# A fourth K pair by seven products in the first iteration of both down stages

## The chip, the cores and the metric

The kernel runs on one core of a Trainium2 chip. The metric is the device time of one execution in microseconds (us). Engines are named as the profile names them: PE is TensorE (PEld its weight loads), DVE is VectorE, ACT is ScalarE, POOL is GpSimd, and SP issues the weight DMAs.

## What is computed

One layer of a macaron decoder block on 256 tokens of width 2048, all in float32. The part that the change touches is the second half of each SwiGLU, the product with `w_down` (5632 x 2048), which occurs twice, in `ffn1` and `ffn2`:

```python
def swiglu(x, w_up, w_down):
    g, u = jnp.split(x @ w_up, 2, axis=-1)
    return (jax.nn.silu(g) * u) @ w_down

h = h + 0.5 * rms_norm(swiglu(rms_norm(h, ffn1_pre[l]), ffn1_up[l], ffn1_down[l]), ffn1_post[l])
...
h = h + 0.5 * rms_norm(swiglu(rms_norm(h, ffn2_pre[l]), ffn2_up[l], ffn2_down[l]), ffn2_post[l])
```

## The kernel before

**Three products for one.** PE works on rounded operands (`fp32r`). Each float32 operand is split into a rounded part (`_hi`, written by ACT) and the rest (`_lo`, written by DVE as raw minus hi), and a product is three matmuls: hi x hi, hi x lo, lo x hi (lines 779 to 781, or `three`, lines 870 to 872).

**Groups.** Weights arrive in groups of 256 rows (two K tiles of 128) by 512 columns, 512 KB each, into four slots of `w_raw`; group n uses slot n % 4. For each group SP issues the load (line 572) once DVE has split the group four earlier; ACT rounds it (`w_hi`, line 1260) once PE is through with the group four earlier; DVE takes the rest (`w_lo`, line 1641); PE multiplies it with both token tiles (2 K tiles x 2 token tiles x 3 = 12 matmuls of 128x128 by 128x512). ACT, DVE and SP each work through their own program in order. In the loops of ACT and DVE, step n splits group n+4.

**The down stage.** `down0` and `down1` have two iterations (i = 0, 1). One iteration computes two strips of 512 output columns, A and B, over all 22 pairs k of K tiles, in 44 groups; a tuple per iteration, `DOWN_A` and `DOWN_B`, says at which group number which pair is taken for strip A or B. Steps 40 to 43 of an iteration go tile by tile.

**Quads.** For the pairs named in `DOWN_QUADS`, as (group of A, group of B, k), the four 2x2 block products of strips A and B are done by seven block products in place of eight (`down_products`, lines 927 to 975): 7 x 3 = 21 matmuls where two plain groups take 24. The price is on DVE and ACT. At DVE step ng-4, `down_sum13` (line 1850, 128x1024) waits for `t_used`, that is for PE's last product of the quad before, since there is a single `dt_raw`, `dt_hi`, `dt_lo`; then come the weight split of group ng and `down_sum24` (lines 1858 and 1860, 128x512 each). The split of group nu is only 512 wide. Steps ng-3 and ng-2 each have a `dt_lo` of 128x1024 (line 1906), behind ACT's `dt_hi` (line 1399). PE waits for the first `dt_lo` before its product into bank3, for the second before that into bank2:

```python
pe.wait_ge(t_split, 2 * down_quad(f, i, j) + 1)
p7 = three(bank[3][:, :], *s(2), *tt(1), first, last)
p5 = three(bank[1][:, :], *s(0), *tt(0), first, last)
pe.wait_ge(t_split, 2 * down_quad(f, i, j) + 2)
p6 = three(bank[2][:, :], *s(1), *tt(2), first, last)
```

**The activations' splits.** The hidden activations (`act_raw`) come in 11 strips p of 512, strip p serving pairs k = 2p and 2p+1. `HIDDEN[0]` says at which step of the first iteration a strip is split: ACT writes `act_hi` (line 1341, two instructions), DVE `act_lo` (line 1680, two instructions). For strips 8, 9 and 10 (`D_STRIPS`, the strips of the quads) DVE first forms four sums (`hidden_sums`, lines 1873 to 1876), and a step later ACT and DVE split those (`ds_hi` line 1382, `ds_lo` line 1882). A product of pair k waits on `hid_split` for strip k//2. DVE's order within a step (lines 1896 to 1913):

```python
if n + SLOTS in DQ_A[i]: down_sum13(f, i, DQ_A[i][n + SLOTS])
rest_group(sec, i, n)
if n + SLOTS in DQ_A[i]: down_sum24(f, i, DQ_A[i][n + SLOTS])
if n in DT_AT[i]: ...            # dt_lo
if n in HIDDEN[i]: ...           # hidden_sums for strips 8, 9, 10, then hidden_lo
if n - 1 in HIDDEN[i] and HIDDEN[i][n - 1] in D_STRIPS: hidden_sums_lo(f, HIDDEN[i][n - 1])
```

After the last quad DVE combines the banks (`d_u`, lines 1917 to 1925), and at step `A_LAST` it reads strip A's accumulators (lines 1928 and 1929).

Of the kernel before, what the change touches and what calls it, by code (L numbers as in the profile page):

```python
# [62 lines left out]
def numbered(first, ks):  # L63

    return {first + j: k for j, k in enumerate(ks)}


DOWN_QUADS = (((24, 25, 16), (29, 30, 17), (33, 34, 18)),
              ((4, 5, 16), (9, 10, 17), (14, 15, 18), (18, 19, 19), (22, 23, 20), (26, 27, 21)))
DOWN_A = ({**numbered(0, range(4)), **numbered(8, (4, 5)), **numbered(12, (6, 7)), **numbered(16, (8, 9)),  # L70
           **numbered(20, (10, 11)), **numbered(26, (12, 13)), **numbered(31, (14, 15)), **numbered(35, (19, 20, 21))},
          {**numbered(0, (8, 9, 10)), **numbered(6, (12, 13, 14)), 11: 15, 12: 11, **numbered(28, range(8))})
DOWN_B = ({**numbered(4, range(4)), **numbered(10, (4, 5)), **numbered(14, (6, 7)), **numbered(18, (8, 9)),
           **numbered(22, (10, 11)), 28: 12, **numbered(38, (13, 14, 15, 19, 20, 21))},
          {3: 8, 13: 9, **numbered(16, (10, 11)), **numbered(20, (12, 13)), **numbered(24, (14, 15)), **numbered(36, range(8))})
A_LAST = tuple(max(a) for a in DOWN_A)
HIDDEN = ({2: 2, 5: 3, 8: 4, 11: 5, 13: 6, 15: 7, 18: 8, 24: 9, 32: 10}, {})
D_STRIPS = (8, 9, 10)
D_K0 = 2 * D_STRIPS[0]
NDK = 2 * len(D_STRIPS)  # L80
NDQ = sum(map(len, DOWN_QUADS))

# [69 lines left out]
def hybrid_trunk(nc, t, out):  # L152
# [17 lines left out]
    with ctx:  # L170
# [313 lines left out]
        def down_quad(f, i, j):  # L484

            return NQUAD * NST * (f + 1) + NDQ * f + sum(map(len, DOWN_QUADS[:i])) + j

# [5 lines left out]
        QUAD_UP = {nu: j for j, (ng, nu, k) in enumerate(QUADS)}  # L493
        DQ_A = [{ng: j for j, (ng, nu, k) in enumerate(quads)} for quads in DOWN_QUADS]
        DQ_B = [{nu: j for j, (ng, nu, k) in enumerate(quads)} for quads in DOWN_QUADS]
        T_SLOT = (1, 0, 1)
# [17 lines left out]

        DT_AT = [{ng - 3 + pair: (j, pair) for j, (ng, nu, k) in enumerate(quads) for pair in range(2)} for quads in DOWN_QUADS]

# [51 lines left out]
        def _(sp):  # L568
# [40 lines left out]
            def down_loads(f):  # L609
                for i in range(CH // 2):  # L610
                    source = {n: (k, 0) for n, k in DOWN_A[i].items()}
                    source.update({n: (k, 1) for n, k in DOWN_B[i].items()})
                    for ng, nu, k in DOWN_QUADS[i]:
                        source[ng], source[nu] = (k, 0), (k, 1)
# [633 lines left out]
        def _(act):  # L1248
# [89 lines left out]
            def hidden_hi(f, p):  # L1338
                wait_turned_in(act, f, p)
                for m in range(MT):  # L1340
                    last = act.activation(act_tile(act_hi, p, m), raw_tile(p, m), ACT.Copy)
                last.then_inc(hid_rounded, 1)
# [35 lines left out]
            def sums_hi(f, p):  # L1378

                j = 2 * D_STRIPS.index(p)  # L1380
                act.wait_ge(ds_summed, len(D_STRIPS) * f + D_STRIPS.index(p) + 1)
                act.activation(ds_hi[:, :, j:j + 2, :], ds_raw[:, :, j:j + 2, :], ACT.Copy).then_inc(ds_rounded, 1)
# [7 lines left out]
            def down_strips(f, i):  # L1390

                sec, final = f"down{f}", i == CH // 2 - 1
                for n in range(2 * GF - SLOTS):
                    round_group(sec, i, n)
                    if n in DT_AT[i]:
# [3 lines left out]
                        act.activation(dt_hi[:, both, :], dt_raw[:, both, :], ACT.Copy).then_inc(t_rounded, 1)  # L1399
                    if n in HIDDEN[i]:  # L1400
                        hidden_hi(f, HIDDEN[i][n])
                    if n - 1 in HIDDEN[i] and HIDDEN[i][n - 1] in D_STRIPS:
                        sums_hi(f, HIDDEN[i][n - 1])
                    if n == DOWN_QUADS[i][-1][0]:
# [223 lines left out]
        def _(dve):  # L1628
# [233 lines left out]
            def hidden_sums(f, p):  # L1862

                j, pairs = 2 * D_STRIPS.index(p), 2
                wait_turned_in(dve, f, p)

                def s(y):
                    return ds_raw[:, y, j:j + pairs, :].rearrange("p j (q i) -> p j q i", i=SQ)

                def a(m, kk):  # L1870
                    return raw_tile(p, m)[:, kk:2 * pairs:2]

                link(dve.tensor_tensor(s(0), a(1, 0), a(1, 1), ALU.subtract))
                link(dve.tensor_tensor(s(1), s(0), a(0, 0), ALU.subtract))
                dve.tensor_tensor(s(2), a(0, 0), a(1, 0), ALU.subtract)
                dve.tensor_tensor(s(3), a(0, 1), s(1), ALU.add).then_inc(ds_summed, 1)
# [13 lines left out]
            def down_strips(f, i):  # L1890
# [4 lines left out]
                for n in range(2 * GF - SLOTS):  # L1895
# [5 lines left out]
                    if n in DT_AT[i]:  # L1901
# [5 lines left out]
                                          ALU.subtract).then_inc(t_split, 1)  # L1907
                    if n in HIDDEN[i]:
                        if HIDDEN[i][n] in D_STRIPS:
                            hidden_sums(f, HIDDEN[i][n])  # L1910
# [410 lines left out]
```

## Time and profile before

| what | us |
|---|---|
| three runs, median (lowest to highest) | 2372.98 (2372.71 to 2373.5) |
| the profiled execution | 2372.41 |
| its span, first to last instruction | 2370.6 |
| PE busy in the span | 2356.8 (99%) |
| DVE busy | 1750.5 (74%) |
| ACT busy | 1243.2 (52%) |

The profile is of one execution; its span leaves out 1.8 us around the instructions. The first iteration of `down0` runs from 472.5 to about 591 us of the span, that of `down1` from 2128.7 to about 2247. In the timelines a matmul's row lasts 0.39 us from its start to its modelled end, but the next one starts 0.23 us after it. A DVE row's duration likewise reaches over the start of the next.

### The profile page before, as it was taken

Reading aid. Unit: us, or ns where it says so; the run is one execution under the profiler, and the core shown is the slowest. Engines: PE = TensorE matmul, PEld = TensorE weight load, DVE = VectorE, ACT = ScalarE, POOL = GpSimd, SP = SyncE. Lnnn points to the kernel's source line nnn. Section 1 sums busy time; section 2 is a strip of 40 time slices with the busy share of each in tenths; the row PEclk is TensorE's granted clock in tenths of the full one; section 3 lists DMA queues with packets and bytes.
Section 4 is the critical chain, followed back from the end, with each engine's and each line's share of the span. In section 5 each row is a group of like instructions: output and inputs, shape, how many; then the busy total and the mean of one; then the engine's idle time right before and its main releaser. Section 6 shows DMA issues by size and latency. Waiting matters only on the chain. (4 is left out here: it accounts for less than half of the span.)

```text
span 2370.6 us, 33710 instructions
## 1 busy us (share of the span) xinstructions
PE 2356.8 (99%) x10613; PEld 1945.0 (82%) x10613; DVE 1750.5 (74%) x2057; ACT 1243.2 (52%) x1490; POOL 205.9 (9%) x398
## 2 busy tenths in 40 slices
PE   9999999999999999999999999999999999999998
PEld 7888888888888888888888888888888888888887
DVE  6999999978876555655545545555799999997886
ACT  6555555555545454444544444444655555555553
POOL 1212112110000000000000000000021211211000
PEclk9999999999999999999999999999999999999999
DMA  7766666665675555565656566655666666666665
GB/s 236 220 212 203 216 219 222 212 221 191 209 240 172 163 175 178 159 188 157 204 187 196 190 198 193 189 185 194 207 213 227 206 218 207 221 212 214 204 204 195
DMA packets 266605, 477.44 MB, mean 201 GB/s; under 512 B 21152, under 2 KB 54608, under 8 KB 265392
## 3 DMA queue, kind: packets, MB, share of 16 engines
q1 hardware_dynamic: 252752, 453.04, 59.6%
q0 software_dynamic: 13616, 23.53, 3.0%
q8 instruction: 35, 0.57, 0.1%
q14 instruction: 26, 0.21, 0.0%
q10 hardware_dynamic: 176, 0.07, 0.0%
HBM read 460.84 MB, written 4.19 MB: 196 GB/s over the span
## 5 line engine op out<-in xcount | busy, mean ns | idle before, releaser
L1260 ACT ACTIVATE w_hi<-w_raw 128x1024 fp32r<-128x1024 f32 (+1 forms) x848 | 863.6, 1021 | 985.9 <-PE acc L781 732.1
L1641 DVE TENSOR_TENSOR w_lo<-w_raw,w_hi 128x1024 fp32r<-128x1024 f32 (+1 forms) x848 | 991.8, 1172 | 507.5 <-ACT w_hi L1260 503.0
L779 PE MATMUL acc<-w_hi,xT_hi 128*128 128x512 f32 x1552 | 609.2, 393 | 1.0 <-DVE w_lo L1641 1.0
L781 PE MATMUL acc<-w_hi,xT_lo 128*128 128x512 f32 x1552 | 604.4, 389 | 0.0
L780 PE MATMUL acc<-w_lo,xT_hi 128*128 128x512 f32 x1552 | 604.1, 389 | 0.0
L779 PEld LDWEIGHTS acc<-w_hi,xT_hi 128*128 128x128 f32 x1552 | 291.4, 188 | 63.0 <-issue 2.5
L781 PEld LDWEIGHTS acc<-w_hi,xT_lo 128*128 128x128 f32 x1552 | 291.3, 188 | 61.1
L780 PEld LDWEIGHTS acc<-w_lo,xT_hi 128*128 128x128 f32 x1552 | 291.5, 188 | 59.3
L696 POOL DMA_DIRECT2D act_raw<-blocks x352 | 174.9, 497 | 736.4 <-DVE blocks L1978 647.5
L779 PE MATMUL acc<-w_hi,act_hi 128*128 128x512 f32 x560 | 218.2, 390 | 0.1
L780 PE MATMUL acc<-w_lo,act_hi 128*128 128x512 f32 x560 | 217.9, 389 | 0.0
L781 PE MATMUL acc<-w_hi,act_lo 128*128 128x512 f32 x560 | 217.9, 389 | 0.0
L870 PE MATMUL acc<-w_hi,xT_hi 128*128 128x512 f32 x460 | 178.9, 389 | 0.0
L871 PE MATMUL acc<-w_lo,xT_hi 128*128 128x512 f32 x460 | 178.9, 389 | 0.0
L872 PE MATMUL acc<-w_hi,xT_lo 128*128 128x512 f32 x460 | 178.9, 389 | 0.0
L2024 DVE TENSOR_TENSOR t_lo<-t_raw,t_hi 128x1024 fp32r<-128x1024 f32 x120 | 146.2, 1218 | 0.0
L1458 ACT ACTIVATE t_hi<-t_raw 128x1024 fp32r<-128x1024 f32 x120 | 126.8, 1057 | 31.1 <-DVE t_raw L1829 22.1
L779 PEld LDWEIGHTS acc<-w_hi,act_hi 128*128 128x128 f32 x560 | 105.2, 188 | 22.6 <-DVE act_lo L1680 0.9
L781 PEld LDWEIGHTS acc<-w_hi,act_lo 128*128 128x128 f32 x560 | 105.1, 188 | 21.8
L780 PEld LDWEIGHTS acc<-w_lo,act_hi 128*128 128x128 f32 x560 | 105.1, 188 | 21.8
L871 PEld LDWEIGHTS acc<-w_lo,xT_hi 128*128 128x128 f32 x460 | 86.3, 188 | 18.0
L870 PEld LDWEIGHTS acc<-w_hi,xT_hi 128*128 128x128 f32 x460 | 86.3, 188 | 17.9
(269 smaller groups left out, 2601.4 us busy)
## 6 DMA issues: line engine op xcount, KB each, us to landing
w_raw<-in_ffn_up_dram SPq DMA_DIRECT2D x352, 512.0 KB, 4.2
w_raw<-in_ffn_down_dram SPq DMA_DIRECT2D x176, 512.0 KB, 4.2
w_raw<-in_w_gate_dram SPq DMA_DIRECT2D x96, 512.0 KB, 3.8
w_raw<-in_w_in_dram SPq DMA_DIRECT2D x72, 512.0 KB, 3.6
w_raw<-in_w_in_dram SPq DMA_DIRECT2D x128, 256.0 KB, 2.9
w_raw<-in_w_ret_out_dram SPq DMA_DIRECT2D x32, 512.0 KB, 3.7
w_raw<-in_w_out_dram SPq DMA_DIRECT2D x32, 512.0 KB, 4.2
act_raw<-blocks POOLq DMA_DIRECT2D x352, 32.0 KB, 3.8
```

What stands on the lines that cost most here:

```text
L696: pool.dma_start(act_raw[to * SQ:(to + 1) * SQ, ds(p, 1), q, :, :, :].rearrange("p a m k i -> p (a m) k i"), blocks[q * SQ:(q + 1) * SQ, t ...
L779: pe.matmul(pair[m][:, :], xh, wh, start=(first and kk == 0), stop=False)
L780: pe.matmul(pair[m][:, :], xh, wl, start=False, stop=False)
L781: mm = pe.matmul(pair[m][:, :], xl, wh, start=False, stop=(last and kk == KG - 1))
L870: pe.matmul(dst, xh, wh, start=start, stop=False)
L871: pe.matmul(dst, xh, wl, start=False, stop=False)
L872: return pe.matmul(dst, xl, wh, start=False, stop=stop)
L1260: act.activation(w_hi[:, s, cols], w_raw[:, s, cols], ACT.Copy).then_inc(w_rounded, 1)
L1458: act.activation(t_pair(t_hi, j, pair), t_pair(t_raw, j, pair), ACT.Copy).then_inc(t_rounded, 1)
L1641: dve.tensor_tensor(w_lo[:, s, cols], w_raw[:, s, cols], w_hi[:, s, cols].bitcast(f32), ALU.subtract).then_inc(w_split, 1)
L2024: dve.tensor_tensor(t_pair(t_lo, j, pair), t_pair(t_raw, j, pair), t_pair(t_hi, j, pair).bitcast(f32), ALU.subtract).then_inc(t_split, 1)
```

## The change

The first iteration of both down stages gets a fourth quad, k = 19, and the quads move to groups 22, 26, 30 and 34. The plain pairs of A and B move around them (strip 10's first pair, k = 20, stays at group 36, which now comes directly after a quad; before, k = 19 lay between). The splits of the activations' strips 5 to 10 move from steps 11, 13, 15, 18, 24, 32 to 10, 12, 14, 16, 23, 33. The second iteration is untouched. The whole diff:

```diff
-DOWN_QUADS = (((24, 25, 16), (29, 30, 17), (33, 34, 18)),
+DOWN_QUADS = (((22, 23, 16), (26, 27, 17), (30, 31, 18), (34, 35, 19)),
               ((4, 5, 16), (9, 10, 17), (14, 15, 18), (18, 19, 19), (22, 23, 20), (26, 27, 21)))
 DOWN_A = ({**numbered(0, range(4)), **numbered(8, (4, 5)), **numbered(12, (6, 7)), **numbered(16, (8, 9)),
-           **numbered(20, (10, 11)), **numbered(26, (12, 13)), **numbered(31, (14, 15)), **numbered(35, (19, 20, 21))},
+           **numbered(20, (10, 11)), **numbered(28, (12, 13)), **numbered(32, (14, 15)), **numbered(36, (20, 21))},
           {**numbered(0, (8, 9, 10)), **numbered(6, (12, 13, 14)), 11: 15, 12: 11, **numbered(28, range(8))})
 DOWN_B = ({**numbered(4, range(4)), **numbered(10, (4, 5)), **numbered(14, (6, 7)), **numbered(18, (8, 9)),
-           **numbered(22, (10, 11)), 28: 12, **numbered(38, (13, 14, 15, 19, 20, 21))},
+           **numbered(24, (10, 11)), **numbered(38, (12, 13, 14, 15, 20, 21))},
           {3: 8, 13: 9, **numbered(16, (10, 11)), **numbered(20, (12, 13)), **numbered(24, (14, 15)), **numbered(36, range(8))})
 A_LAST = tuple(max(a) for a in DOWN_A)
-HIDDEN = ({2: 2, 5: 3, 8: 4, 11: 5, 13: 6, 15: 7, 18: 8, 24: 9, 32: 10}, {})
+HIDDEN = ({2: 2, 5: 3, 8: 4, 10: 5, 12: 6, 14: 7, 16: 8, 23: 9, 33: 10}, {})
```

**DVE around the split of strip 9.** First the order before, from the second `dt_raw` sum of the first iteration to the two `dt_lo` of that quad (the sum's line is L1850, a weight split L1641, strip 9's sums end with L1876, its split is L1680, the split of its sums L1882):

```order
L1876 TENSOR_TENSOR ds_raw<-act_raw,ds_raw 128x256
L1680 TENSOR_TENSOR act_lo<-act_raw,act_hi 128x4x128 x2
L1850 TENSOR_TENSOR dt_raw<-w_raw 128x1024
L1641 TENSOR_TENSOR w_lo<-w_raw,w_hi 128x1024
L1858 TENSOR_TENSOR dt_raw<-dt_raw,w_raw 128x512
L1860 TENSOR_TENSOR dt_raw<-dt_raw,w_raw 128x512
L1882 TENSOR_TENSOR ds_lo<-ds_raw,ds_hi 128x4x256
L1641 TENSOR_TENSOR w_lo<-w_raw,w_hi 128x512
L1906 TENSOR_TENSOR dt_lo<-dt_raw,dt_hi 128x1024
L1641 TENSOR_TENSOR w_lo<-w_raw,w_hi 128x1024
L1906 TENSOR_TENSOR dt_lo<-dt_raw,dt_hi 128x1024
```

Now the same quad in the changed kernel, from its last sum on:

```order
L1860 TENSOR_TENSOR dt_raw<-dt_raw,w_raw 128x512
L1641 TENSOR_TENSOR w_lo<-w_raw,w_hi 128x512
L1906 TENSOR_TENSOR dt_lo<-dt_raw,dt_hi 128x1024
L1873 TENSOR_TENSOR ds_raw<-act_raw 128x256
L1874 TENSOR_TENSOR ds_raw<-ds_raw,act_raw 128x256
L1875 TENSOR_TENSOR ds_raw<-act_raw 128x256
L1876 TENSOR_TENSOR ds_raw<-act_raw,ds_raw 128x256
L1680 TENSOR_TENSOR act_lo<-act_raw,act_hi 128x4x128 x2
L1641 TENSOR_TENSOR w_lo<-w_raw,w_hi 128x1024
L1906 TENSOR_TENSOR dt_lo<-dt_raw,dt_hi 128x1024
L1882 TENSOR_TENSOR ds_lo<-ds_raw,ds_hi 128x4x256
```

Strip 9's four sums and its two `act_lo` stood ahead of the sum L1850 that waits for PE; now they stand behind it, between the quad's first and second `dt_lo`.

**DVE around the split of strip 10.** In the changed kernel, from the second `dt_lo` of the last quad (groups 34 and 35) on:

```order
L1906 TENSOR_TENSOR dt_lo<-dt_raw,dt_hi 128x1024
L1641 TENSOR_TENSOR w_lo<-w_raw,w_hi 128x1024
L1873 TENSOR_TENSOR ds_raw<-act_raw 128x256
L1874 TENSOR_TENSOR ds_raw<-ds_raw,act_raw 128x256
L1875 TENSOR_TENSOR ds_raw<-act_raw 128x256
L1876 TENSOR_TENSOR ds_raw<-act_raw,ds_raw 128x256
L1680 TENSOR_TENSOR act_lo<-act_raw,act_hi 128x4x128 x2
```

These rows read the same before, behind the second `dt_lo` of the quad at groups 33 and 34. What differs is on PE: before, that quad was followed by group 35 (k = 19, strip 9) and then by group 36 (k = 20, strip 10); now the quad at 34 and 35 is followed by group 36 at once.

## Rows read from the trace of the kernel before

**Rows 1.** The page: busy time and instructions of the engines, and PE's granted clock.
```profile
PE 2356.8 (99%) x10613; PEld 1945.0 (82%) x10613; DVE 1750.5 (74%) x2057; ACT 1243.2 (52%) x1490; POOL 205.9 (9%) x398
...
PEclk9999999999999999999999999999999999999999
```
**Rows 2.** Waits of PE, the longest: us in total, times, longest.
```profile
PE acc L1036 <- DVE gate_sb L2067: 2.0, 1, 2.0
PE acc L779 <- DVE xT_lo L1658: 1.2, 3, 0.6
```
**Rows 3.** Windows, first iteration of down0: us, then busy us per engine, PEclk, DMA share, GB/s.
```profile
472.50:537.80 65.30, 65.30 (x288) 54.05 (x289) 49.43 (x58) 36.36 (x43) 8.51 (x17) 1.00 0.62 207
537.80:565.70 27.90, 27.90 (x125) 23.10 (x124) 26.46 (x33) 17.86 (x20) 0.00 (x0) 1.00 0.63 213
565.70:591.00 25.30, 25.30 (x113) 20.97 (x112) 20.64 (x28) 13.13 (x17) 0.00 (x0) 1.00 0.53 181
```
**Rows 4.** Timeline of PE: start us, us; groups 31 and 32, then the quad 33, 34.
```profile
555.49 0.39 PE L779 MATMUL acc<-w_hi,act_hi 128*128 128x512 f32 x1
...
560.93 0.39 PE L870 MATMUL bank<-w_hi,act_hi 128*128 128x512 f32 x1
...
565.69 0.39 PE L779 MATMUL acc<-w_hi,act_hi 128*128 128x512 f32 x1
```
**Rows 5.** Timeline of PEld, the same quad: loads of the bank3 and bank2 products, then group 35.
```profile
562.74 0.19 PEld L870 LDWEIGHTS bank<-dt_hi,ds_hi 128*128 128x128 f32 x1
...
564.10 0.19 PEld L870 LDWEIGHTS bank<-dt_hi,ds_hi 128*128 128x128 f32 x1
...
565.46 0.19 PEld L779 LDWEIGHTS acc<-w_hi,act_hi 128*128 128x128 f32 x1
```
**Rows 6.** Timeline of DVE: from the quad's first sum to behind strip 10's split.
```profile
555.69 1.23 DVE L1850 TENSOR_TENSOR dt_raw<-w_raw 128x1024 f32<-128x1024 f32 x1 [1.23 <-PE acc L872]
...
559.90 1.22 DVE L1906 TENSOR_TENSOR dt_lo<-dt_raw,dt_hi 128x1024 fp32r<-128x1024 f32 x1
561.03 1.22 DVE L1641 TENSOR_TENSOR w_lo<-w_raw,w_hi 128x1024 fp32r<-128x1024 f32 x1
562.16 1.22 DVE L1906 TENSOR_TENSOR dt_lo<-dt_raw,dt_hi 128x1024 fp32r<-128x1024 f32 x1
563.30 1.22 DVE L1641 TENSOR_TENSOR w_lo<-w_raw,w_hi 128x1024 fp32r<-128x1024 f32 x1
564.44 0.42 DVE L1873 TENSOR_TENSOR ds_raw<-act_raw 128x256 f32<-128x256 f32 x1
...
566.02 1.29 DVE L1680 TENSOR_TENSOR act_lo<-act_raw,act_hi 128x512 fp32r<-128x512 f32 x2
567.23 1.22 DVE L1641 TENSOR_TENSOR w_lo<-w_raw,w_hi 128x1024 fp32r<-128x1024 f32 x1
```
**Rows 7.** Timeline of all engines, start of down0: PE waits for an activation strip.
```profile
471.05 1.29 DVE L1680 TENSOR_TENSOR act_lo<-act_raw,act_hi 128x512 fp32r<-128x512 f32 x2
...
471.70 0.19 PEld L872 LDWEIGHTS acc<-w_hi,xT_lo 128*128 128x128 f32 x1
471.93 0.39 PE L872 MATMUL acc<-w_hi,xT_lo 128*128 128x512 f32 x1
...
472.39 0.19 PEld L779 LDWEIGHTS acc<-w_hi,act_hi 128*128 128x128 f32 x1 [0.50 <-DVE act_lo L1680]
...
472.72 0.39 PE L780 MATMUL acc<-w_lo,act_hi 128*128 128x512 f32 x1
```
**Rows 8.** Timeline of DVE in down1: the same quad's first sum, strip 10's sums and split.
```profile
2211.94 1.22 DVE L1850 TENSOR_TENSOR dt_raw<-w_raw 128x1024 f32<-128x1024 f32 x1 [0.79 <-PE acc L872]
...
2222.28 1.28 DVE L1680 TENSOR_TENSOR act_lo<-act_raw,act_hi 128x512 fp32r<-128x512 f32 x2
```
**Rows 9.** Timeline of DVE, then of ACT: group 30's split frees slot 2; group 34 lands.
```profile
549.23 0.69 DVE L1641 TENSOR_TENSOR w_lo<-w_raw,w_hi 128x512 fp32r<-128x512 f32 x1
...
554.54 0.63 ACT L1260 ACTIVATE w_hi<-w_raw 128x512 fp32r<-128x512 f32 x1 [1.13 <-DMA w_raw<-in_ffn_down_dram]
```
**Rows 10.** PE's last matmul, and two windows behind it (PEclk third from the end).
```profile
2361.80 0.39 PE L781 MATMUL acc<-w_hi,act_lo 128*128 128x512 f32 x1
...
2366.00:2367.00 1.00, 0.00 (x0) 0.00 (x0) 1.00 (x3) 0.00 (x0) 0.00 (x0) 1.00 0.07 29
2367.00:2368.00 1.00, 0.00 (x0) 0.00 (x0) 1.00 (x2) 0.00 (x0) 0.00 (x0) 0.55 1.01 391
```

## The prediction

> **What bounds the kernel now.** I read the page first: PE is busy 2356.8 of 2370.6 us, and its longest waits, at the start of the kernel, are 2.0 and 1.2 us [rows 1, 2]. So PE bounds the kernel nearly everywhere: a matmul less is time less, and a microsecond that PE waits is a microsecond more. Next the windows of the first iteration of `down0`: PE is busy all the time in all three, at granted clock 1.00 (the 2.4 GHz level), but DVE is busy 49.43 of 65.30 us ahead of the quads, 26.46 of 27.90 us among them and 20.64 of 25.30 us behind them [rows 3]. Among the quads DVE is within 5% of PE, and this is where the change adds DVE work. An average does not say whether DVE is late, so the rest is read from the timelines, instruction by instruction.
>
> **Pace of PE.** From 555.49 to 560.93 us PE does two plain groups, 24 matmuls: 5.44 / 24 = 0.2267 us each. From 560.93 to 565.69 it does a quad: 4.76 us, 21 matmuls at the same pace [rows 4]. Quads four groups apart therefore repeat every 5.44 + 4.76 = 10.20 us on PE.
>
> **Part 1, the matmuls removed.** Pair 19 takes 21 matmuls in place of 24, once in each of two down stages: 6 x 0.2267 = 1.36 us less, on the bounding engine. This is all that the change can gain. The Trainium skill ("TensorE: Matmul & The Clock Gate", Back-to-back issue gap) gives N/2.4 + 2.5 ns, 216 ns for 512 columns; by it the sum would have 1.30 us here. The rows have 0.2267 us, which is what I take.
>
> **Part 2, the fourth quad's own DVE work.** By the rows a cycle of a quad four groups after another runs thus. The first sum starts 0.20 us after PE has begun the next group (555.69 against 555.49), since it waits for the quad before; the first `dt_lo` starts at 559.90, the second at 562.16 and ends at 562.16 + 1.22 = 563.38 [rows 4, 6]. PE's weight loads that need them are at 562.74 and 564.10 [rows 5]. So both are in time, the second by 0.72 us. Before, DVE does strip 10's split after this, ends it with its last weight split of the cycle, and in the second iterations quads follow each other at the same distance. A cycle without a strip's split thus costs nothing: cover is the 10.20 us of PE, of which the chain from the first sum to the weight split behind the second `dt_lo` takes 564.44 - 555.69 = 8.75 us. ACT is busy 17.86 of 27.90 us and its added roundings stay hidden [rows 3]. The weights come in time too: group 30's slot was free at 549.92 and group 34 there was rounded from 554.54, 4.6 us later, though it was waited for [rows 9]; with quads 10.20 us apart and the half-width split done some 4.4 us into a cycle (559.90 against 555.49), the slot lands at about 9.0, over 1 us ahead of the next sum.
>
> **Part 3, strip 9's split moves behind the waiting sum.** It stood in step 24, ahead of the sum that waits for PE. Now it stands in step 23, between the two `dt_lo` of the quad at 26. Its price is that of strip 10's same six instructions: 567.23 - 564.44 = 2.79 us [rows 6]. The second `dt_lo` then ends at 563.38 + 2.79 = 566.17 on the clock of those rows, while the load that needs it is due at 564.10: 2.07 us late. How lateness turns into lost time is read at the start of `down0`: `act_lo` ended at 471.05 + 1.29 = 472.34; the load was due at 471.93 (0.23 us after that of 471.70), so it was 0.41 us late; the matmul of 472.72 would have come at 471.93 + 2 x 0.2267 = 472.38, so 0.34 us was lost [rows 7]. Lost time is lateness less 0.07. **Stall 1 is 2.00 us in each down stage.** Nothing on DVE can run ahead to take it away, since the chain starts with a sum that waits for PE.
>
> What is late next: behind the second `dt_lo` DVE has strip 9's `ds_lo` and a weight split, 1.14 us each (561.03 to 562.16 for one such [rows 6]). It comes free at about 8.75 + 2.79 + 1.14 = 12.68 us after the first sum started; PE ends the quad 10.20 + 2.00 = 12.20 us after the cycle's start. The next sum is thus some 0.5 us later than it could be, and the second `dt_lo` of the quad at 30 has about 0.25 us in hand in place of 0.72. No stall, but it is thin. The cycle after that is back on PE's pace.
>
> **Part 4, strip 10's split against the group that follows the last quad.** Relative to the cycle's start nothing moves on DVE: before, strip 10's `act_lo` ended at 566.02 + 1.29 = 567.31, that is 11.82 us after 555.49 [rows 4, 6]. Before, its first user, group 36, came a plain group later than the quad's end, its load due at 565.46 + 2.72 = 568.18, 0.87 us later. Now group 36 follows the quad at once, and its load is due at the place of 565.46 [rows 5]: 567.31 - 565.46 = 1.85 us late. **Stall 2 is 1.78 us in each down stage.** Behind it DVE's combinations of the banks have the plain groups 36 to 43 as cover, as before.
>
> **Part 5, the rest.** Strips 5 to 8 are split one or two steps earlier, where DVE is busy 49.43 of 65.30 us [rows 3]; strip 8 stays two steps ahead of the first quad's sum. Nothing for them. In `down1` the same chain from the first sum to the end of strip 10's split takes 2222.28 + 1.28 - 2211.94 = 11.62 us against 567.31 - 555.69 = 11.62 in `down0` [rows 6, 8], so both stalls count twice.
>
> **The sum.** -1.36 + 2 x (2.00 + 1.78) = +6.20 us. On the profiled execution's own 2372.41 us that gives 2378.6; the median of the runs shown is 0.57 us higher, 2372.98, and with it 2379.2 us, which I predict. Bounds: if none of it stalled, 2371.6; with 0.3 us of error in each of four stalls, 2378.0 to 2380.4. A measurement of this kernel can tell about 0.2%, 4.7 us, from no change; the forecast is +0.26%, slower, but not far over that line, which lies at 2377.7.
>
> **The rivals.**
> - *Nothing waits.* The place is the load at 564.10 and the one at 565.46. If the six instructions of strip 9 took under 0.72 us there, or DVE were ahead of the chain, both stalls would vanish and 2372.98 - 1.36 = 2371.6 us be left, no slower than before. For it speaks that PE never waited in this stage; against it that the six took 2.79 us and that the chain starts with PE's own signal [rows 5, 6]. 5%.
> - *One of the two stalls only.* 2372.98 - 1.36 + 4.00 = 2375.6, or with the other 2375.2. For it: part 3 adds up a sequence which no row shows whole, while part 4's sequence is there row by row, only its user moved. 8%.
> - *Both, but each some 0.5 us shorter*, because PE can hold more back than at the start of `down0`: 2377.2. 4%.
> - *A cascade.* The quad at 30 has 0.25 us in hand. If a DMA or ACT takes 0.5 to 1.5 us more there, 1 to 3 us come on top: 2380 to 2382. For it: one weight load was already waited for 1.13 us by ACT [rows 9]. 10%.
> - *The clock falls.* In the rows the clock still was 1.00 in 2366 to 2367 us, 4 us behind the last matmul at 2361.80, and 0.55 in the next microsecond [rows 10]. Stalls of 2 us are shorter than that, so the rows speak against a fall. If it fell in each of four stalls and stayed for 5 us, half of each would be lost: 4 x 2.5 = 10 us, 2389. The Trainium skill ("TensorE: Matmul & The Clock Gate", HAM oscillation) has waits of PE throw the array back to the half rate again and again. [...] 2%.
> - That the change does not do what it says is out: the order of the changed kernel shows six PE matmuls fewer and the new place of strip 9.
>
> **How the numbers follow.** The forecast has the remaining 71%. It and the cascade span 2378.0 to 2382; with the shorter stalls the range is 2377.0 to 2382.0, which leaves out 15% of cases and a few unknown ones. Slower by over 0.2%: the forecast less the part that falls under 2377.7 (some 5%), the cascade and the clock: 78%. Within 0.2%: the other cases and that part, 21%. Faster by over 0.2% (under 2368.2) has no case, since the gain is at most 1.36 us: 1%.
>
> **What would show it.** PE's matmuls down by 6. A wait of PE of about 2 us in front of the product into bank2 of the quad at 26 (released by DVE's `dt_lo`, L1906), near 546 us, once per down stage; a wait of about 1.8 us at L779 released by `act_lo` (L1680), behind the quad at 34, once per stage; from there on everything about 3.1 us later than before, and 6.2 us from `down1` on. On DVE the next sum (L1850) after stall 1 with little or no idle ahead of it. The clock at 1.00 throughout. The prediction is wrong if PE has no wait on L1906, or if its waits at L1680 do not grow beyond the 0.5 us of before.

## The result and the profile after

| | before | changed |
|---|---|---|
| median of 9 runs, us | 2372.90 | 2379.43 |
| lowest to highest | 2372.50 to 2373.57 | 2378.71 to 2381.53 |
| profiled execution, us | 2372.41 | 2379.94 |
| its span | 2370.6 | 2377.8 |

The ratio is 1.0028, 95% interval 1.0019 to 1.0036: slower, by 6.5 us at the medians, where 2379.2 was forecast. The page of the changed kernel, its busy times and clock, answers to [rows 1]:

```profile
PE 2357.5 (99%) x10607; PEld 1944.3 (82%) x10607; DVE 1758.4 (74%) x2067; ACT 1245.8 (52%) x1494; POOL 204.0 (9%) x398
...
PEclk9999999999999999999999999999999999999999
```

Six matmuls fewer (10613 to 10607), 8 us more on DVE, the clock as it was. Where the time is lost stands in the waits of the changed kernel, first PE's, then its weight loads' (us in total, times, longest); before, PE's waits were the 2.0 and 1.2 us of [rows 2] and smaller ones:

```profile
PE bank L870 <- DVE dt_lo L1906: 3.5, 2, 1.7
PE acc L779 <- DVE act_lo L1680: 3.3, 3, 1.5
PE acc L1036 <- DVE gate_sb L2067: 2.0, 1, 2.0
```
```profile
PEld acc L779 <- DVE act_lo L1680: 5.1, 4, 1.9
PEld bank L870 <- DVE dt_lo L1906: 4.3, 2, 2.2
```

Both waits that were forecast are there, one of each per down stage. The remaining, short waits for `act_lo` (two at the loads, one at PE) are those at the starts of the stages. The same wait has two sizes in these views: the first one is 1.74 us at PE and 2.16 us at the load. A matmul's row reaches 0.16 us past the start of the next one, and a load row ends 0.04 us ahead of the next load. What is lost is neither of the two: it is read from the starts of matmuls, below.

**The first wait.** DVE in the changed kernel, `down0`, the quad at 26, from its first sum to the next quad's, answering to [rows 6]:

```profile
537.92 1.23 DVE L1850 TENSOR_TENSOR dt_raw<-w_raw 128x1024 f32<-128x1024 f32 x1 [2.17 <-PE acc L872]
...
542.13 1.22 DVE L1906 TENSOR_TENSOR dt_lo<-dt_raw,dt_hi 128x1024 fp32r<-128x1024 f32 x1
543.26 0.42 DVE L1873 TENSOR_TENSOR ds_raw<-act_raw 128x256 f32<-128x256 f32 x1
...
544.85 1.28 DVE L1680 TENSOR_TENSOR act_lo<-act_raw,act_hi 128x512 fp32r<-128x512 f32 x2
546.05 1.22 DVE L1641 TENSOR_TENSOR w_lo<-w_raw,w_hi 128x1024 fp32r<-128x1024 f32 x1
547.19 1.21 DVE L1906 TENSOR_TENSOR dt_lo<-dt_raw,dt_hi 128x1024 fp32r<-128x1024 f32 x1
548.33 1.22 DVE L1882 TENSOR_TENSOR ds_lo<-ds_raw,ds_hi 128x1024 fp32r<-128x1024 f32 x1
549.46 1.21 DVE L1641 TENSOR_TENSOR w_lo<-w_raw,w_hi 128x1024 fp32r<-128x1024 f32 x1
550.60 1.22 DVE L1850 TENSOR_TENSOR dt_raw<-w_raw 128x1024 f32<-128x1024 f32 x1
```

DVE idles 2.17 us for PE's signal and then has no gap until the next sum. The six instructions of strip 9 take 546.05 - 543.26 = 2.79 us, and the second `dt_lo` ends at 548.40. PE's loads in the same cycle, answering to [rows 5]:

```profile
546.11 0.19 PEld L872 LDWEIGHTS bank<-dt_hi,ds_lo 128*128 128x128 f32 x1
548.46 0.19 PEld L870 LDWEIGHTS bank<-dt_hi,ds_hi 128*128 128x128 f32 x1 [2.16 <-DVE dt_lo L1906]
548.57 0.19 PEld L871 LDWEIGHTS bank<-dt_lo,ds_hi 128*128 128x128 f32 x1
```

The waiting load came 0.06 us after the `dt_lo`; it was due at 546.11 + 0.23 = 546.34. PE's matmuls give the loss. The groups after the quads at 22 and at 26 begin at the first and the last of these rows; the second is the product that waited:

```profile
537.72 0.39 PE L779 MATMUL acc<-w_hi,act_hi 128*128 128x512 f32 x1
...
548.46 0.50 PE L870 MATMUL bank<-dt_hi,ds_hi 128*128 128x512 f32 x1 [1.74 <-DVE dt_lo L1906]
...
549.95 0.39 PE L779 MATMUL acc<-w_hi,act_hi 128*128 128x512 f32 x1
```

That is 12.23 us in place of 10.20: 2.03 us lost (forecast 2.00). At the second matmul behind the wait it was 2.00; the other 0.03 is a slightly slower pace of the next matmuls. The next sum stood at 550.60, 0.65 us after PE's new group, where 0.20 is the least that a wait for PE leaves [rows 4, 6]. So the quad at 30 had little in hand: its second `dt_lo` ended at 558.29, its load came at 558.57 on PE's pace, and it did not wait.

**The second wait.** The quad at 34, then group 36. DVE, then PE:

```profile
560.35 1.23 DVE L1850 TENSOR_TENSOR dt_raw<-w_raw 128x1024 f32<-128x1024 f32 x1 [0.93 <-PE acc L872]
...
570.69 1.29 DVE L1680 TENSOR_TENSOR act_lo<-act_raw,act_hi 128x512 fp32r<-128x512 f32 x2
```
```profile
570.13 0.39 PE L872 MATMUL acc<-dt_hi,act_lo 128*128 128x512 f32 x1
572.03 0.50 PE L779 MATMUL acc<-w_hi,act_hi 128*128 128x512 f32 x1 [1.52 <-DVE act_lo L1680]
572.37 0.40 PE L780 MATMUL acc<-w_lo,act_hi 128*128 128x512 f32 x1
...
575.61 0.39 PE L779 MATMUL acc<-w_hi,act_hi 128*128 128x512 f32 x1
```

`act_lo` ended at 571.98, 11.63 us after the cycle's first sum (before: 11.62 [rows 6]). The matmul at 572.37 would have come at 570.13 + 2 x 0.2267 = 570.58: 1.79 us lost (forecast 1.78). The matmuls behind it come up to 0.24 us apart before PE is back at 0.2267. The one at 575.61 is the 16th after 570.13 and would have come at 570.13 + 16 x 0.2267 = 573.76, so in the end this wait lost 1.85 us.

The windows of the changed kernel's `down0` answer to [rows 3]. Among the quads PE is now busy 29.46 of 31.20 us (94%) and DVE 29.98 (96%). DVE's share is the higher one now, though an average of this kind does not say where a wait ends last:

```profile
472.50:537.80 65.30, 65.02 (x287) 53.69 (x287) 50.42 (x59) 37.15 (x44) 8.51 (x17) 1.00 0.64 214
537.80:569.00 31.20, 29.46 (x131) 24.06 (x130) 29.98 (x34) 19.60 (x22) 0.00 (x0) 1.00 0.55 185
569.00:594.00 25.00, 23.48 (x104) 19.09 (x103) 20.00 (x30) 12.01 (x17) 0.00 (x0) 1.00 0.49 165
```

### The profile page after: what moved, and what is told of

Its sections match the earlier page's. It is cut to its first block and busy times, and to the rows that moved or that the text cites. A ratio compares the mean times of both kernels' runs of the same rounds, so it can differ in the third digit from the quotient of the medians.

```text
span 2377.8 us, 33723 instructions
## 1 busy us (share of the span) xinstructions
PE 2357.5 (99%) x10607; PEld 1944.3 (82%) x10607; DVE 1758.4 (74%) x2067; ACT 1245.8 (52%) x1494; POOL 204.0 (9%) x398
## 5 line engine op out<-in xcount | busy, mean ns | idle before, releaser
L1641 DVE TENSOR_TENSOR w_lo<-w_raw,w_hi 128x1024 fp32r<-128x1024 f32 (+1 forms) x848 | 990.8, 1171 | 500.3 <-ACT w_hi L1260 495.9
L781 PEld LDWEIGHTS acc<-w_hi,xT_lo 128*128 128x128 f32 x1552 | 291.3, 188 | 61.1
L780 PEld LDWEIGHTS acc<-w_lo,xT_hi 128*128 128x128 f32 x1552 | 291.5, 188 | 59.0
L779 PE MATMUL acc<-w_hi,act_hi 128*128 128x512 f32 x544 | 212.2, 390 | 3.5 <-DVE act_lo L1680 3.3
L780 PE MATMUL acc<-w_lo,act_hi 128*128 128x512 f32 x544 | 211.7, 389 | 0.0
L781 PE MATMUL acc<-w_hi,act_lo 128*128 128x512 f32 x544 | 211.7, 389 | 0.0
L870 PE MATMUL acc<-w_hi,xT_hi 128*128 128x512 f32 x460 | 178.9, 389 | 0.0
L870 PEld LDWEIGHTS acc<-w_hi,xT_hi 128*128 128x128 f32 x460 | 86.3, 188 | 18.0
L872 PEld LDWEIGHTS acc<-w_hi,xT_lo 128*128 128x128 f32 x460 | 86.3, 188 | 17.9
```

Of the source, the lines that this page charges most:

```text
L779: pe.matmul(pair[m][:, :], xh, wh, start=(first and kk == 0), stop=False)
L780: pe.matmul(pair[m][:, :], xh, wl, start=False, stop=False)
L781: mm = pe.matmul(pair[m][:, :], xl, wh, start=False, stop=(last and kk == KG - 1))
L870: pe.matmul(dst, xh, wh, start=start, stop=False)
L872: return pe.matmul(dst, xl, wh, start=False, stop=stop)
L1641: dve.tensor_tensor(w_lo[:, s, cols], w_raw[:, s, cols], w_hi[:, s, cols].bitcast(f32), ALU.subtract).then_inc(w_split, 1)
```

## The experiments

Eight kernels. The first four below were timed beside the kernel before at 2372.71 us (33 runs), the other four beside it at 2372.88 us (26 runs). The differences asked for are 1 to 7 us, and an interval of a ratio is about 2 us to either side. So beside the time stands what the trace says of the place.

**Strip 9 split ahead of the quads.** In the changed kernel; strips 6 to 8 move forward too, to make room:

```diff
-HIDDEN = ({2: 2, 5: 3, 8: 4, 10: 5, 12: 6, 14: 7, 16: 8, 23: 9, 33: 10}, {})
+HIDDEN = ({2: 2, 5: 3, 8: 4, 10: 5, 11: 6, 12: 7, 13: 8, 16: 9, 33: 10}, {})
```

> The changed kernel with strip 9 split at step 16, ahead of the quads, and strips 6 to 8 a little earlier (11, 12, 13); strip 10 stays at step 33. Theory (two separate waits of PE, one for strip 9's split between the two dt_lo, one for strip 10's split behind the last quad): the first goes, the second stays, so against before -1.36 + 2 x 1.78 = +2.2 us, 2375.1 us; PE has no wait at L870 for dt_lo, and two of about 1.9 us (weight load) at L779 for act_lo. Rival A (four quads four groups apart overload DVE wherever the strips are split, since the DVE work is the same): about 2379.4 us as in the changed kernel, with waits at L870 still there. Rival B (most of the loss is in the strip 10 wait and the first would be made good later): still about 2379.

Measured 2375.22 us (1.0012, 1.0003 to 1.0021). PE has no wait for `dt_lo`. The waits of its loads for `act_lo` stay (here in `down0` and `down1`):

```profile
569.47 0.19 PEld L779 LDWEIGHTS acc<-w_hi,act_hi 128*128 128x128 f32 x1 [1.94 <-DVE act_lo L1680]
...
2227.06 0.19 PEld L779 LDWEIGHTS acc<-w_hi,act_hi 128*128 128x128 f32 x1 [1.94 <-DVE act_lo L1680]
```

The two waits are separate, and the first goes when the splits of strips 6 to 9 stand earlier. That it hangs on strip 9 is shown by the run with strip 9 alone moved, below. Both rivals fall: they had 2379.

**Strip 10 one step earlier.** In the changed kernel:

```diff
-HIDDEN = ({2: 2, 5: 3, 8: 4, 10: 5, 12: 6, 14: 7, 16: 8, 23: 9, 33: 10}, {})
+HIDDEN = ({2: 2, 5: 3, 8: 4, 10: 5, 12: 6, 14: 7, 16: 8, 23: 9, 32: 10}, {})
```

> The changed kernel with strip 10's split one step earlier, 32 in place of 33, ahead of one weight split of 1.14 us on VectorE. Theory: stall 2 shrinks by those 1.14 us, 1.78 to 0.64 us in each stage, stall 1 stays at 2.00; against before -1.36 + 4.00 + 1.28 = +3.9 us, 2376.8 us. Rival (strip 10's split has a fixed price in DVE's load and is not a matter of the distance to its first user): unchanged, 2379.4 us. The loads of group 36 should wait about 0.8 us for act_lo in place of 1.94.

Measured 2377.17 us (1.0019, 1.0010 to 1.0028). The wait shrank by the one weight split that strip 10 passed, 1.94 to 0.80 us, and the first wait stayed. The rival, 2379.4 us, is out:

```profile
548.40 0.19 PEld L870 LDWEIGHTS bank<-dt_hi,ds_hi 128*128 128x128 f32 x1 [2.16 <-DVE dt_lo L1906]
570.84 0.19 PEld L779 LDWEIGHTS acc<-w_hi,act_hi 128*128 128x128 f32 x1 [0.80 <-DVE act_lo L1680]
```

**The kernel before, with groups 35 and 36 exchanged.**

```diff
-           **numbered(20, (10, 11)), **numbered(26, (12, 13)), **numbered(31, (14, 15)), **numbered(35, (19, 20, 21))},
+           **numbered(20, (10, 11)), **numbered(26, (12, 13)), **numbered(31, (14, 15)), **numbered(35, (20, 19, 21))},
```

> The kernel before (three quads, its own steps for the splits), with only the pairs of groups 35 and 36 exchanged: k = 20, the first user of strip 10, comes directly behind the quad at 33 and 34. Not an instruction more or less on any engine. Theory: PE waits 1.78 us for strip 10's act_lo in each down stage, +3.6 us against before, 2376.5 us, and no other wait is new. Rival (the fourth quad's own work on DVE is what makes strip 10 late): with three quads nothing changes, 2372.9 us.

Measured 2376.63 us (1.0016, 1.0007 to 1.0025).

```profile
567.83 0.19 PEld L779 LDWEIGHTS acc<-w_hi,act_hi 128*128 128x128 f32 x1 [1.95 <-DVE act_lo L1680]
```

The second wait arises without a fourth quad, and with no instruction added anywhere: it is the distance from strip 10's split to its first user. The rival, with nothing changed, is out.

**All strips split ahead of the quads.**

```diff
-HIDDEN = ({2: 2, 5: 3, 8: 4, 10: 5, 12: 6, 14: 7, 16: 8, 23: 9, 33: 10}, {})
+HIDDEN = ({2: 2, 4: 3, 6: 4, 7: 5, 8: 6, 9: 7, 10: 8, 13: 9, 16: 10}, {})
```

> The changed kernel with all splits of strips ahead of the first quad: strips 2 to 10 at steps 2, 4, 6, 7, 8, 9, 10, 13 and 16. Theory: both waits go and the six matmuls less remain, -1.36 us against before, 2371.5 us, with no wait of PE for dt_lo and none for act_lo beyond the 0.5 us at the start of each stage. Rival A (the quads' own DVE work is too dense at four groups apart): a wait at L870 stays and the time is above 2374. Rival B (the strips moved ahead make DVE late there, where it is busy 49 of 65 us): new waits of PE at L779 for w_lo, or of DVE for weights, over 1 us a stage, 2374 or more.

Measured 2371.81 us (0.9996, 0.9987 to 1.0005): by the time alone no difference from before. By the trace neither wait is there; all that PE's matmuls wait for `act_lo` in the whole kernel is 0.2 us at the start of a stage:

```profile
PE acc L779 <- DVE act_lo L1680: 0.2, 1, 0.2
```

From its first to its last product with `act_lo`, `down0` takes 706.53 - 473.38 = 233.15 us and `down1` 231.92, against 233.85 and 232.61 before: 1.4 us less, the six matmuls. The fourth quad's own DVE work is covered. Rival A is out, with no wait at L870; so is rival B, with PE's waits for `w_lo` at 1.0 us in the whole kernel, as before. DVE in that kernel, two quads in a row, idles 1.37 us for PE ahead of each sum:

```profile
547.95 1.23 DVE L1850 TENSOR_TENSOR dt_raw<-w_raw 128x1024 f32<-128x1024 f32 x1 [1.37 <-PE acc L872]
...
558.15 1.22 DVE L1850 TENSOR_TENSOR dt_raw<-w_raw 128x1024 f32<-128x1024 f32 x1 [1.37 <-PE acc L872]
```

**The kernel before, strip 9 between its quad's two `dt_lo`.** The quads stay five groups apart there.

```diff
-HIDDEN = ({2: 2, 5: 3, 8: 4, 11: 5, 13: 6, 15: 7, 18: 8, 24: 9, 32: 10}, {})
+HIDDEN = ({2: 2, 5: 3, 8: 4, 11: 5, 13: 6, 15: 7, 18: 8, 26: 9, 32: 10}, {})
```

> The kernel before (three quads) with strip 9's split moved from step 24 to step 26, between the two dt_lo of its quad at 29, the same place in the order that it has in the changed kernel, but with that quad five groups behind the one before. Theory (lateness is counted from PE's signal to the load that needs the dt_lo, so the fifth group's 2.72 us are cover): the second dt_lo ends about 2.79 us later and is still in time, no wait, 2372.7 us. Rival (the place between the two dt_lo is what costs, whatever the distance of the quads): about 2 us of wait at L870 per stage, 2376.7 us.

Measured 2373.07 us (1.0001, 0.9992 to 1.0010). No wait for `dt_lo`: the second one, at 551.86, ends at 553.08, and its load at 553.53 comes on PE's pace.

```profile
551.86 1.22 DVE L1906 TENSOR_TENSOR dt_lo<-dt_raw,dt_hi 128x1024 fp32r<-128x1024 f32 x1
```
```profile
553.53 0.19 PEld L870 LDWEIGHTS bank<-dt_hi,ds_hi 128*128 128x128 f32 x1
```

The same six instructions at the same place in the order cost nothing with one plain group more between the quads, and the rival is out. One part of the expectation missed: the second `dt_lo` was to end about 2.79 us later than before, and it ended at about the same time (before: 552.10 + 1.22 = 553.32). Before, that quad's sum came straight behind strip 9's split, with no wait for PE; here it starts 2.11 us earlier, on PE's signal. Its row before, then in this run:

```profile
544.50 1.22 DVE L1850 TENSOR_TENSOR dt_raw<-w_raw 128x1024 f32<-128x1024 f32 x1
```
```profile
542.39 1.22 DVE L1850 TENSOR_TENSOR dt_raw<-w_raw 128x1024 f32<-128x1024 f32 x1 [0.66 <-PE acc L872]
```

**Strip 10 two steps earlier.** In the changed kernel:

```diff
-HIDDEN = ({2: 2, 5: 3, 8: 4, 10: 5, 12: 6, 14: 7, 16: 8, 23: 9, 33: 10}, {})
+HIDDEN = ({2: 2, 5: 3, 8: 4, 10: 5, 12: 6, 14: 7, 16: 8, 23: 9, 31: 10}, {})
```

> The changed kernel with strip 10's split two steps earlier, 31 in place of 33, between the two dt_lo of the last quad. Theory: the wait of 1.78 us at L779 for act_lo goes, and a wait of 2.00 us at L870 for the last quad's second dt_lo takes its place; stall 1 stays; against before -1.36 + 2 x (2.00 + 2.00) = +6.6 us, 2379.4 us, with four waits of about 2.1 us at the weight loads of L870. Rival (an earlier split of strip 10 is simply better, as step 32 was): below 2377 us.

Measured 2379.77 us (1.0029, 1.0018 to 1.0040). The wait for `act_lo` is gone, and a second one for `dt_lo` stands in its place, so an earlier split is not simply better:

```profile
548.41 0.19 PEld L870 LDWEIGHTS bank<-dt_hi,ds_hi 128*128 128x128 f32 x1 [2.16 <-DVE dt_lo L1906]
570.85 0.19 PEld L870 LDWEIGHTS bank<-dt_hi,ds_hi 128*128 128x128 f32 x1 [2.16 <-DVE dt_lo L1906]
```

**Strip 9 one step later.** In the changed kernel:

```diff
-HIDDEN = ({2: 2, 5: 3, 8: 4, 10: 5, 12: 6, 14: 7, 16: 8, 23: 9, 33: 10}, {})
+HIDDEN = ({2: 2, 5: 3, 8: 4, 10: 5, 12: 6, 14: 7, 16: 8, 24: 9, 33: 10}, {})
```

> The changed kernel with strip 9's split one step later, 24 in place of 23, behind the second dt_lo of the quad at 26. Theory: that quad's wait goes, but VectorE then has strip 9's 2.79 us, a weight split and ds_lo (1.14 us each) ahead of the next sum, which comes 2.5 us late; the second dt_lo of the quad at 30 is 1.76 us late, 1.69 us lost; stall 2 stays; against before -1.36 + 2 x (1.69 + 1.78) = +5.6 us, 2378.3 us. The wait at L870 appears about one quad later, near 557 us in place of 548. Rival (the loss came only from the split standing between the two dt_lo): only stall 2 is left, 2375.1 us.

Measured 2378.98 us (1.0025, 1.0015 to 1.0036). The wait moved to the quad at 30 as expected, but it has three parts, since the weight split of the second group and the first `dt_lo` were late too:

```profile
554.43 0.19 PEld L870 LDWEIGHTS acc<-w_hi,ds_hi 128*128 128x128 f32 x1 [0.47 <-DVE w_lo L1641]
555.57 0.19 PEld L870 LDWEIGHTS bank<-dt_hi,ds_hi 128*128 128x128 f32 x1 [0.60 <-DVE dt_lo L1906]
557.84 0.19 PEld L870 LDWEIGHTS bank<-dt_hi,ds_hi 128*128 128x128 f32 x1 [1.04 <-DVE dt_lo L1906]
571.23 0.19 PEld L779 LDWEIGHTS acc<-w_hi,act_hi 128*128 128x128 f32 x1 [1.91 <-DVE act_lo L1680]
```

From the matmul at 554.00, the last ahead of these waits, to the one at 559.13 PE does 15 matmuls in 5.13 us, where its pace gives 15 x 0.2267 = 3.40: 1.73 us lost, where 1.69 was expected for a single wait. The rival, 2375.1 us, is out: moved alone, strip 9 takes its wait along. At steps 23 and 24, once the run of quads four groups apart has begun, it costs 2.03 and 1.73 us a stage; other steps between these quads were not tried.

**Five quads.** A version after the theory:

```diff
-DOWN_QUADS = (((24, 25, 16), (29, 30, 17), (33, 34, 18)),
+DOWN_QUADS = (((18, 19, 16), (22, 23, 17), (26, 27, 18), (30, 31, 19), (34, 35, 20)),
...
-           **numbered(20, (10, 11)), **numbered(26, (12, 13)), **numbered(31, (14, 15)), **numbered(35, (19, 20, 21))},
+           **numbered(20, (10, 11)), **numbered(24, (12, 13)), **numbered(28, (14, 15)), 37: 21},
...
-DOWN_B = ({**numbered(4, range(4)), **numbered(10, (4, 5)), **numbered(14, (6, 7)), **numbered(18, (8, 9)),
-           **numbered(22, (10, 11)), 28: 12, **numbered(38, (13, 14, 15, 19, 20, 21))},
+DOWN_B = ({**numbered(4, range(4)), **numbered(10, (4, 5)), **numbered(14, (6, 7)), **numbered(32, (8, 9)),
+           36: 10, **numbered(38, (11, 12, 13, 14, 15, 21))},
...
-HIDDEN = ({2: 2, 5: 3, 8: 4, 11: 5, 13: 6, 15: 7, 18: 8, 24: 9, 32: 10}, {})
+HIDDEN = ({1: 2, 2: 3, 3: 4, 4: 5, 5: 6, 6: 7, 7: 8, 10: 9, 12: 10}, {})
```

> A version after the theory: five quads (k = 16 to 20) at 18, 22, 26, 30 and 34 in the first iteration of both down stages, all strips split ahead of them (steps 1 to 7, 10, 12). Theory: two quads more than before, 4 x 3 x 0.2267 = 2.72 us less on PE, 2370.0 us; the second dt_lo of the first quad is ready some 0.8 us ahead of its load, so no new wait, or one of a few tenths. Rival A (VectorE has no room for all splits in the first 14 steps): waits of PE at L779 for w_lo or at L870 for dt_lo of 1 to 3 us per stage, 2371 to 2375 us. Rival B (the weight loads come late behind the late splits): waits for DMA in front of ACT and PE, over 2372 us.

Measured 2370.06 us (0.9989, 0.9980 to 0.9998): 2.8 us less than before, and the only version whose interval lies below 1. PE does 12 matmuls fewer, waits at no `dt_lo` and has no new wait for `w_lo` or a weight load, so both rivals are out. But the first quad is near the edge. Its second `dt_lo` ends at 524.22, its load is due at 524.99, and DVE is busy 45.44 of the first 46 us of the stage, 99%:

```profile
523.00 1.22 DVE L1906 TENSOR_TENSOR dt_lo<-dt_raw,dt_hi 128x1024 fp32r<-128x1024 f32 x1
```
```profile
472.00:518.00 46.00, 45.74 (x202) 37.51 (x202) 45.44 (x63) 31.27 (x41) 8.51 (x17) 1.00 0.66 218
```

All together, us against the kernel before. The third column is the length of the two down stages in the traces, from the start of the first to the start of the last product with `act_lo`.

| kernel | expected | stages in the trace | medians |
|---|---|---|---|
| changed | +6.2 | +6.4 | +6.5 |
| strip 9 at step 16 | +2.2 | +2.2 | +2.5 |
| strip 10 at step 32 | +3.9 | +4.1 | +4.5 |
| before, groups 35, 36 exchanged | +3.6 | +3.7 | +3.9 |
| all strips early | -1.4 | -1.4 | -0.9 |
| before, strip 9 at step 26 | 0 | 0.0 | +0.2 |
| strip 10 at step 31 | +6.6 | +6.7 | +6.9 |
| strip 9 at step 24 | +5.6 | +5.8 | +6.1 |
| five quads | -2.7 | -2.7 | -2.8 |

## Why the prediction was right

- **The bound.** PE bounds the kernel, and every wait of PE in a down stage came out at the end. In all nine rows of the table the medians lie within 0.6 us, and the stages within 0.2 us, of sums that assume just this.
- **Part 1, the six matmuls: confirmed**, -1.4 us in the stages of the kernel with all strips early, -2.7 us for the twelve of five quads. The pace between quads without a wait is still 10.20 us (558.15 - 547.95 above), so 0.2267 us for a matmul was the price to take.
- **Part 2, the quad's own DVE work at nothing: confirmed.** The cover was named as 10.20 us of PE against a chain of 8.75 us; with the strips out of the way, DVE's idle ahead of a sum is 1.37 us. The difference of the two is 1.45, and a DVE row lasts 0.08 us past the start of the next.
- **Part 3, strip 9: confirmed in place and size**, 2.03 us lost in `down0` where 2.00 was forecast. Splitting strips 6 to 9 earlier took the wait away, and moving strip 9 alone moved it to another quad. The neighbour that was called thin, the quad at 30, held, with its sum some 0.45 us later than PE's signal allowed and 0.28 us in hand (0.25 was forecast).
- **Part 4, strip 10: confirmed in place, a little short in size**: 1.79 us at the second matmul behind the wait against 1.78, and 1.85 in the end. The exchange of two groups in the kernel before shows it apart from everything else.
- **The weights**: in the rows of PE no wait is put down to a weight DMA. ACT still waits for some loads among the quads, as before (29 waits, 29.1 us, for `w_down` in the whole kernel, against 26 and 27.0); PE's rows show nothing of it.
- **What was off.** The changed kernel is 6.5 us slower at the medians and 6.4 in its stages, not 6.2. The 0.2 us in the stages are in the two waits: the prediction took lost time as lateness less 0.07 us, which it had read at the second matmul behind a wait [rows 7]. The matmuls after that still lose a little, so that the waits cost 2.03 and 1.85 us in place of 2.00 and 1.78, in `down0` and `down1` alike: -1.36 + 2 x (2.03 + 1.85) = +6.40. What is left at the medians, 0.1 us, is far within the interval. In the profiled execution the span grew by 7.2 us. The 0.8 us beyond the stages lie where nothing was changed, 0.35 of it ahead of the first weight product (9.04 against 8.69), a place that varies from 8.55 to 9.21 over the ten traces.
- **Rivals.** One stall only, and nothing waits: out, both waits are in the trace. Both, but each some 0.5 us shorter: out, they were 0.03 and 0.07 us longer than forecast. A cascade: out in the changed kernel; the run with strip 9 at step 24 shows that a late sum does make the quad at 30 wait. A late DMA or ACT there, the cause that the rival named, was not tried. The clock: out, granted 1.00 in all three windows of the stage, with PE idle for 1.74 and 1.52 us in two of them.

## What to carry to other kernels

Where a chain of instructions on one engine starts with a wait for the bounding engine, count the time from that signal to the first consumer that needs the chain's end; whatever is put in between costs its length less the slack, though the engine is far from fully busy on average. Work without a near deadline (here the activations' splits) belongs ahead of such a run of chains, and its first user should not be moved next to it without that count. The gain of 3 matmuls (0.68 us) in a stage of some 234 us was real, and the placement of two strips' splits, each under 3 us of DVE work, cost over five times as much (3.88 us).

## What the runs showed of the hardware beyond that

- After a wait of PE the first load and its matmul start together, 0.05 to 0.06 us behind the end of the DVE row, and the second load follows 0.11 us later in place of 0.23 (548.46, 548.57).
- At the second matmul behind a wait the loss is thus some 0.06 us less than the lateness: `dt_lo` ended 2.06 us behind the due time of its load (548.40 and 546.34) and 2.00 was lost, `act_lo` 1.85 (571.98 and 570.13) and 1.79 was lost; [rows 7] had 0.41 and 0.34. That does not last. The next matmuls start 0.23 to 0.24 us apart, and within 24 of them the loss is 2.03 of 2.06 and 1.85 of 1.85. What makes them slower is not shown.
- The granted clock stayed at 1.00 around every wait of about 2 us, in the six traces that have them, as in [rows 10] it stayed for 4 us behind the last matmul. The Trainium skill ("TensorE: Matmul & The Clock Gate", HAM oscillation) tells of a kernel whose waits for DMA take the array to its lower clock again and again. Those waits are longer than the ones here; waits of 2 us in a stream that is otherwise dense did not do it in these traces.
